# Expert blocks' rows by an indirect load from a scratch tensor instead of a one-hot product, and a signal of its own for the gate half

## The reference

```python
def clamped_swiglu(hgu):
    gate, up = jnp.split(hgu, 2, axis=-1)
    gate = jnp.minimum(gate, SWIGLU_LIMIT)
    up = jnp.clip(up, -SWIGLU_LIMIT, SWIGLU_LIMIT)
    return gate * jax.nn.sigmoid(SWIGLU_ALPHA * gate) * (up + 1)

xs = xt[row_tok].reshape(NB, MOE_BLOCK, D)      # the rows of each block's tokens
def expert_block(args):
    xb, e = args
    return clamped_swiglu(xb @ w1[e] + b1[e]) @ w2[e] + b2[e]
y = jnp.zeros((T, D)).at[row_tok].add(yb * row_gate[:, None])
```

## Time and profile before

| | |
|---|---|
| median of 3 runs | 2496.36 us (2496.22 to 2497.87) |
| the profiled execution | 2495.2 us |
| its span in the profile | 2493.4 us |
| PE, DVE, ACT, POOL busy | 94%, 42%, 25%, 2% |
| expert weights | 384 loads of 1 MB |

### The profile page before, as it was taken

The page is one execution under the profiler, slowest core; times in us unless marked ns, Lnnn a source line. Parts: engine busy times, 40 slices in busy tenths (PEclk is TensorE's granted clock), DMA queues, the critical chain, the costliest instruction groups (busy, mean ns, idle before and its releaser), DMA issues. The chain is left out here.

```text
span 2493.4 us, 30931 instructions
## 1 busy us (share of the span) xinstructions
PE 2344.1 (94%) x11448; PEld 1251.3 (50%) x11449; DVE 1040.7 (42%) x2256; ACT 633.7 (25%) x1451; POOL 46.0 (2%) x59
## 2 busy tenths in 40 slices
PE   7999899999999989899899789999999999999997
PEld 3545586468745558676786554333333333333332
DVE  3857542153600684766444433232233233223323
ACT  3006632343211353226331321111111111111111
POOL 0000010000000000000001000000000000000000
PEclk9999999999999999999999789999999999999999
DMA  9535611200112002763240149999998998998997
GB/s 374 201 135 203 233 68 43 91 11 35 70 67 80 22 1 101 255 217 136 68 169 34 63 163 405 417 381 377 417 417 350 417 417 348 417 417 346 418 418 307
DMA packets 154250, 567.96 MB, mean 228 GB/s; under 512 B 10832, under 2 KB 12368, under 8 KB 121136
## 3 DMA queue, kind: packets, MB, share of 16 engines
q1 hardware_dynamic: 154160, 566.75, 58.1%
HBM read 565.67 MB, written 1.05 MB: 227 GB/s over the span
## 5 line engine op out<-in xcount | busy, mean ns | idle before, releaser
L2596 PE MATMUL PS<-BIG,PW 128*64 128x512 f32 x2304 | 509.9, 597 | 10.6 <-DMA BIG<-in_w 10.6
L2596 PEld LDWEIGHTS PS<-BIG,PW 128*64 128x64 f32 x2304 | 160.6, 137 | 357.4 <-issue 323.6
L2622 PE MATMUL PS<-BIG,PW 128*64 128x512 f32 x1152 | 255.1, 595 | 8.6 <-ACT PW L2699 8.6
L2785 DVE TENSOR_SCALAR PW<-PS 128x512 f32<-128x512 f32 x36 | 24.9, 691 | 513.0 <-PE PS L2596 513.0
L2696 ACT ACTIVATE PW<-PW 128x512 f32<-128x512 f32 x36 | 22.7, 630 | 757.1 <-DVE PW L2785 757.1
L2622 PEld LDWEIGHTS PS<-BIG,PW 128*64 128x64 f32 x1152 | 79.3, 137 | 161.2 <-issue 144.1
L1062 PE MATMUL PS<-HT,BIG 128*128 128x512 f32 (+1 forms) x448 | 157.5, 507 | 0.0
L682 PE MATMUL PS<-HT,BIG 128*128 128x256 f32 x640 | 139.5, 379 | 2.1 <-PEq L794 2.1
L682 PEld LDWEIGHTS PS<-HT,BIG 128*128 128x128 f32 x640 | 121.4, 190 | 19.1 <-issue 2.7
L1062 PEld LDWEIGHTS PS<-HT,BIG 128*128 128x128 f32 x448 | 85.2, 192 | 65.5 <-issue 56.7
L1407 PE MATMUL PS<-BIG,HT 128*128 128x512 f32 x256 | 110.0, 592 | 0.0
(11 more groups left out here) (469 smaller groups left out, 3137.1 us busy)
## 6 DMA issues: line engine op xcount, KB each, us to landing
BIG<-in_w SPq DMA_DIRECT2D x384, 1024.0 KB, 15.7
BIG<-in_l_w_ada SPq DMA_DIRECT2D x24, 2048.0 KB, 8.3
BIG<-in_l_w_in SPq DMA_DIRECT2D x20, 2048.0 KB, 8.0
BIG<-in_w_ada SPq DMA_DIRECT2D x12, 2048.0 KB, 9.1
BIG<-in_l_w_out SPq DMA_DIRECT2D x8, 2048.0 KB, 8.2
BIG<-in_w_in SPq DMA_DIRECT2D x7, 2048.0 KB, 8.3
BIG<-in_w_out SPq DMA_DIRECT2D x2, 2048.0 KB, 8.1
BIG<-in_l_w_in SPq DMA_DIRECT2D x1, 1792.0 KB, 7.7
```

The source lines that it names most:

```text
L2596: ins = nc.tensor.matmul(PS[64 * g:64 * g + 64, 4 + half, :], xt[:, c % 4, c // 4, :], W[:, c, half * F + g * 512:half * F + g * 512 + 512 ...
L2622: ins = nc.tensor.matmul(PS[64 * g:64 * g + 64, 7, :], at_[:, k % 4, k // 4, :], W[:, 8 + k // 2, k % 2 * D + g * 512:k % 2 * D + g * 512 ...
```

## The change

The normed tokens are also stored to a scratch tensor `token_rows` in HBM, as 512 half rows of 2 KB. A table `row_of` of row numbers, 128 partitions x 49 block columns (MAX_BLOCKS + 1),, is made once: DVE splits each place into block and slot and writes `of_block` (some 18 small instructions, left out below), PE sums the table in 16 products and DVE adds the half-row offset. In the loop POOL copies the block's column of it and issues an indirect load of 128 half rows straight into `xg`, as soon as the rows before have been turned. From block 2 on this replaces the gather on PE, its copy on ACT and the tables on DVE. PE signals the end of the gate half of the first products before the up half of the last chunk, and DVE clamps the gate on that signal; the product with the sigmoid now comes first, and (up + 1) after it.

```diff
+            of_block = take(BIG, rest, 2, K, MAX_BLOCKS + 1)
+            row_of = take(BIG, rest, MAX_BLOCKS + 1).bitcast(U32)
+            row_now = take(BIG, rest, 1).bitcast(U32)
+            token_rows = nc.dram_tensor("token_rows", [2 * LAT, D // 2], F32)
...
+                    sp.wait_ge(*at("d_ready", 4))
+                    sp.dma_start(token_rows.rearrange("(n p g) d -> p n (g d)", n=2, p=P), htok).then_inc(loop["rows_stored"], 16)
...
+                @block.gpsimd
+                def _(pool):
+                    pool.wait_ge(loop["rows_stored"], 16)
+                    pool.wait_ge(loop["row_table_ready"], 1)
+                    n = trips(pool)
+                    with pool.Fori(2, n + 1) as i:
+                        pool.wait_ge(loop["gather_turned"], i)
+                        nc.gpsimd.tensor_tensor(turns[:, 0:1], ones[:, 0:1], ones[:, 0:1], ALU.add)
+                        nc.gpsimd.tensor_copy(row_now, row_of[:, bass.ds(i, 1)]).then_inc(loop["row_ready"], 1)
+                        pool.wait_ge(loop["row_ready"], i - 1)
+                        nc.gpsimd.tensor_tensor(turns[:, 1:2], ones[:, 0:1], ones[:, 0:1], ALU.add)
+                        nc.gpsimd.indirect_dma_start(out=xg, out_offset=None, in_=token_rows[:, :],
+                                                     in_offset=bass.IndirectOffsetOnAxis(ap=row_now, axis=0)).then_inc(loop["rows_landed"], 16)
...
-                    def turn_gathered(i):
+                    def turn_gathered(i, by_dma=True):
-                        pe.wait_ge(loop["gathered_copied"], i + 1)
+                        if by_dma:
+                            pe.wait_ge(loop["rows_landed"], i * 16 - 16)
+                        else:
+                            pe.wait_ge(loop["gathered_copied"], i + 1)
...
+                                if c == 7 and half == 0:
+                                    ins.then_inc(loop["gate_summed"], 1)
...
                     pe.wait_ge(loop["plan_copied"], 1)
+                    pe.wait_ge(loop["slots_split"], 1)
+                    for n in range(2):
+                        for k in range(K):
+                            for g in range(2):
+                                ins = nc.tensor.matmul(PS[64 * g:64 * g + 64, 7, 320:321 + MAX_BLOCKS], eq[:, n, k, :], of_block[:, n, k, :],
+                                                       start=(n + k == 0), stop=(n == 1 and k == K - 1))
+                    ins.then_inc(loop["rows_found"], 1)
...
                     pe.wait_ge(loop["gates_copied"], 1)
-                    second_products(0, 0)
+                    pe.wait_ge(loop["row_table_ready"], 1)
+                    second_products(0, 0, False)
...
-                    gather_next(1)
                     scatter_last(1)
...
                         first_products(i, load)
-                        gather_next(i)
                         scatter_last(i)
...
-                    with act.Fori(0, n) as i:
+                    one_block(0, False)
+                    with act.Fori(1, n) as i:
                         one_block(i)
...
                     tables(lambda x: x)
+                    dve.wait_ge(loop["pick_ready"], 3)
...
+                    ins.then_inc(loop["slots_split"], 1)
+                    link(ts(own[:, 2:3], const("partition"), float(SLOT), None, ALU.is_ge))
+                    dve.wait_ge(loop["rows_found"], 1)
+                    dve.wait_ge(loop["gates_copied"], 1)
+                    ts(row_of, PS[:, 7, 320:321 + MAX_BLOCKS], own[:, 2:3], None, ALU.add).then_inc(loop["row_table_ready"], 1)
...
                     def activation(i):
+                        dve.wait_ge(loop["gate_summed"], i + 1)
+                        nc.vector.tensor_scalar(gate_, PS[:, 4, :], 7.0, None, ALU.min).then_inc(loop["gate_clipped"], 1)
                         dve.wait_ge(used, i * 12 + 8)
-                        nc.vector.tensor_scalar(gate_, PS[:, 4, :], 7.0, None, ALU.min).then_inc(loop["gate_clipped"], 1)
                         nc.vector.tensor_scalar(up, PS[:, 5, :], 7.0, -7.0, ALU.min, ALU.max).then_inc(steps, 1)
-                        dve.wait_ge(steps, i * 8 + 5)
                         dve.wait_ge(loop["gate_clipped"], i + 1)
-                        nc.vector.scalar_tensor_tensor(up, up, 1.0, gate_, ALU.add, ALU.mult).then_inc(steps, 1)
-                        dve.wait_ge(steps, i * 8 + 6)
                         dve.wait_ge(loop["sigmoid_ready"], i + 1)
-                        nc.vector.tensor_tensor(act_, up, sig, ALU.mult).then_inc(loop["act_ready"], 1)
+                        nc.vector.tensor_tensor(gate_, gate_, sig, ALU.mult).then_inc(steps, 1)
+                        dve.wait_ge(steps, i * 4 + 6)
+                        nc.vector.scalar_tensor_tensor(act_, up, 1.0, gate_, ALU.add, ALU.mult).then_inc(loop["act_ready"], 1)
...
-                    dve.wait_ge(loop["gathered"], 2)
-                    tables(lambda x: 8 + x)
...
-                        dve.wait_ge(loop["gathered"], i + 2)
-                        tables(lambda x: i * 8 + (8 + x))
                         outputs(i)
```

More of the change, by code:

```diff
@@ L2402, in routed_experts @@
             norm_rows = take(BIG, rest, D)
+            of_block = take(BIG, rest, 2, K, MAX_BLOCKS + 1)
+            row_of = take(BIG, rest, MAX_BLOCKS + 1).bitcast(U32)
+            row_now = take(BIG, rest, 1).bitcast(U32)
+            turns = take(BIG, rest, 2)
+            token_rows = nc.dram_tensor("token_rows", [2 * LAT, D // 2], F32)
             pw = [0]
@@ L2436, in routed_experts @@
                 "act_copied y_copied scattered bias_used ranked order_ready plan_ready plan_turned plan_copied gate_exp_ready gates_ready gates_spread "
-                "places_ready places_copied gates_turned gates_copied bias2_scaled gather_turned xt_copied".split())}
+                "places_ready places_copied gates_turned gates_copied bias2_scaled gather_turned xt_copied gate_summed rows_stored "
+                "slots_split rows_found row_table_ready row_ready rows_landed".split())}
             with nc.Block() as block:
@@ L2600, in first_products @@
                                 beside()
-                    def gather_next(i):
-                        pe.wait_ge(loop["pick_ready"], i + 3)
-                        gather()
                     def scatter_last(i):
@@ L2609, in scatter_last, with second_products @@
                         scatter()
-                    def second_products(i, load):
+                    def second_products(i, load, by_dma=True):
                         pe.wait_ge(loop["act_ready"], i + 1)
@@ L2615, in second_products @@
                         ins.then_inc(loop["act_turned"], 1)
-                        turn_gathered(i + 1)
+                        turn_gathered(i + 1, by_dma)
                         pe.wait_ge(loop["act_copied"], i + 1)
@@ L2629, in _ @@
                     gather()
-                    turn_gathered(0)
+                    turn_gathered(0, False)
                     pe.wait_ge(loop["ranked"], 1)
@@ L2639, in _ @@
                     ins.then_inc(loop["gates_turned"], 1)
-                    gather_next(0)
+                    pe.wait_ge(loop["pick_ready"], 3)
+                    gather()
                     for n in range(4):
@@ L2692, in _, with one_block @@
                     copy_turned(0)
-                    def one_block(i):
+                    def one_block(i, by_dma=True):
                         act.wait_ge(loop["gate_clipped"], i + 1)
                         nc.scalar.activation(sig, gate_, ACT.Sigmoid, scale=1.702).then_inc(loop["sigmoid_ready"], 1)
-                        copy_gathered(i + 1)
+                        if not by_dma:
+                            copy_gathered(i + 1)
                         act.wait_ge(loop["act_turned"], i + 1)
@@ L2781, in _ @@
                     tables(lambda x: x)
+                    dve.wait_ge(loop["pick_ready"], 3)
+                    whole = own[:, 8:8 + 2 * K].bitcast(I32)
+                    link(nc.vector.tensor_copy(whole, flat(dest0)))
+                    link(ts(whole, whole, SLOT - 1, None, ALU.bitwise_and))
+                    link(nc.vector.tensor_copy(flat(dest), whole))
+                    for n in range(2):
+                        link(tt(eq[:, n, :, :], const("slot_row").unsqueeze(1).to_broadcast([P, K, SLOT]),
+                                dest[:, n, :].unsqueeze(2).to_broadcast([P, K, SLOT]), ALU.is_equal))
@@ new lines, in _ @@
+                    link(tt(dest, dest0, dest, ALU.subtract))
+                    link(ts(dest, dest, 1.0 / SLOT, None, ALU.mult))
+                    link(ts(own[:, 0:1], const("partition"), 2.0, None, ALU.mult))
+                    link(ts(own[:, 1:2], const("partition"), 2.0, float(2 * P), ALU.mult, ALU.add))
+                    for n in range(2):
+                        for k in range(K):
```

(12 more changed lines are left out.)

## The result

The changed kernel takes 2511.38 us (median of 4 runs, 2510.15 to 2513.31) against 2496.29 us for the kernel before beside it: 15.1 us slower, ratio 1.006 with a 95% interval of 1.0042 to 1.0077. The profiled execution has a span of 2508.9 us, 15.5 above the span of before. These are lines of the page of the changed kernel; they answer to the earlier trace rows; the fourth is new, and the last line is the kernel before's counterpart of the fifth.

The account below looks back on a forecast made before the run. The weight stream on the DMA engines (417 GB/s, 30.2 us an expert, plus stops) was taken as the bound; loads +20.4, start +2.3, stops -7.0, end -1.4 sum to +14.3 us, forecast 2510 us, range 2497 to 2530.

Parts of the forecast that it names:

- the terms 2.3 - 7.0 - 1.4: All but the loads: later start of the stream +2.3 us, shorter stops -7.0, shorter end behind the last chunk -1.4.
- the one distance that the forecast named: Time between two resumptions of SP's weight loading after stops, six experts apart: up from 192.0 to about 194.7 us.
- The price of a load: Each block's 262 KB indirect load takes 0.68 us of the 16 DMA engines; 30 count, +20.4 us.
- The free load: Rival: the loads ride beside the weight stream at no cost, so -6 us, 2490 us; chance 0.10.
- the dear one: Rival: POOL-written descriptors and an extra queue hold the engines up to 2.3 us a load, 2559 us; chance 0.07.
- The stops: At four halts of the weight stream PE comes 1.43 us earlier, -5.7 us; with another -1.3 at the first, -7.0.
- the catch-up at the first: At the stream's first stop PE will now have caught up after the start: another -1.3 us.
- The setup: Ahead of the loop, 16 products (3.5 us) and table work delay PE 3.7 us; the stream starts +2.3 us later.
- The end: Behind the last weight chunk, the rest of the kernel shortens by 1.4 us.
- The signal's failure: Rival: the gate half's early signal does not help and transposes start at the old time, 2517 us; chance 0.10.
- The fall of the clock: Rival: PE's waits in each chunk drop TensorE to half clock, 35 us at four stops and the end, 2545; chance 0.03.
- PE idle on DMA about 5 us per block: Sign expected in the profile: PE waits for weights before the first products, in place of 10.6 us in all.

Follow-up runs that it names:

- pair with half chunks: Only half of each weight chunk loaded from the second expert on: kernel before 2478.68 us (ratio 0.9933), changed kernel 2429.21 us (ratio 0.9731).
- none, one and two loads: Changed kernel with each indirect load of the loop removed, kept as it is, or issued twice: 2489.0, 2511.38 and 2530.05 us.
- plain loads by SP: Kernel before with one more SP load of 128 rows of 2 KB behind each expert's 12 chunks: 2513.32 us, ratio 1.0072.
- the kernel without loads: Changed kernel without the indirect load in the loop and the wait for it, xg keeping block 1's rows: 2489.0 us, ratio 0.9969.
- with the old activation: Kernel before with PE's gather moved behind chunk 3 of the first products, without the early gate signal: 2519.72 us, ratio 1.0094.
- the two profiles with the gather moved: Kernel before with PE's gather moved behind chunk 3 of the first products, plus the early gate signal: 2493.47 us, and 2494.18 us when repeated.

## Why the prediction was right

The forecast was 2510, measured 2511.4; its sum, +14.3 us, is what the loop stretch of the profiles shows. The mechanism held; that the number fits to 0.1 us is in part luck. By the loop stretches the loads cost 18.2 us where 20.4 were forecast, and everything else gave back 3.9 where the terms 2.3 - 7.0 - 1.4 make 6.1: two misses of 2.2 us that cancel. By the medians the two are 22.4 and 6.9.

- **What binds.** As predicted: the DMA at 417 GB/s between the stops, and distances between resumptions up by 3.1, 3.6 and 1.7 us, 8.4 in sum. The sum forecast for six, seven and six loads that count, less 1.43 at each stop, is 8.6; the one distance that the forecast named, at 2.7, is the one that fell shortest of it. The pair with half chunks shows it from the other side.
- **The price of a load.** Taken as 0.68 us from rows of the same width. The line through none, one and two loads gives 18 to 22 us for 30 that count, 0.6 to 0.75; the queue's 1.0% of the span gives 0.7 and the plain loads by SP 0.69. The free load (0.10) and the dear one (0.07) are both excluded. The Trainium skill ("DMA: Bandwidth & Descriptors", section "Anatomy of one DMA — SWDGE (gpsimd) path") gives a load about 2.0 us of fixed time and lays it to completion latency. The runs agree: held on the engines it would have made 78 us (the estimate of the forecast), and they show 18 to 22. The loads landed 7.0 us after issue, in a stretch with some 20 us to spare.
- **The stops.** They shrank by 42.4 - 33.3 = 9.1 us. Forecast were 7.0 by PE's gain and the catch-up at the first, and four loads hidden in them, 2.7 more: 9.7. Without the loads they shrank by 42.4 - 36.5 = 5.9, so the loads hid 3.2 us in them. PE's gain of 1.44 us a block was forecast as 1.43.
- **The setup, mis-sized.** Forecast +2.3 with 3.7 us of delay on PE. The changed kernel's start (PE):

```profile
1500.78 1.14 PE L2664 MATMUL PS<-BIG,PW 128*64 128x49 f32 x32
...
1507.72 0.60 PE L2637 MATMUL PS<-CONST,PW 128*128 128x128 f32 x4
...
1522.59 7.92 PE L2621 MATMUL PS<-BIG,PW 128*64 128x512 f32 x28
```

The 16 products took 1.14 us, not 3.5: I had halved the duration of one with its drain, but with 64 weight columns and 49 data columns their 32 records issue every 0.04 us. From expert 1's issue to the transposes it is 13.5 us, 1.0 more than before. Then a thing that I had not counted: some of the products after 1522.6 run at the 1.2 GHz level. This is the window, beside one of the loop (the kernel before has 1.00 in the first, as shown above):

```profile
1516.00:1528.00 12.00, 10.28 (x60) 5.61 (x60) 6.73 (x8) 0.00 (x0) 0.00 (x0) 0.86 0.98 377
```
```profile
2079.00:2096.00 17.00, 13.24 (x57) 3.39 (x56) 0.46 (x1) 0.00 (x0) 0.00 (x0) 1.00 1.01 417
```

Chunk 0 of block 1 is used 3.3 us after its first product where 2.1 were before, and SP issues expert 2 at 1525.86. The forecast was about 1526, 3.7 us of work later than before; it came so by 1.0 us of work, 1.1 of clock and 1.2 by which expert 1's issue itself was later in this profile (1494.2 against 1493.0). That time is right by luck. By the first resumption the whole start is +1.9, in which there are also the first stop, 2.9 us shorter, and the price of the first loads; without loads it is -0.6, as the forecast's 2.3 of setup less 2.7 at that stop makes -0.4.
- **The end.** Forecast -1.4 behind the last weights. These are the last expert's eighth chunk, before and after:

```profile
2466.01 1.94 PE L2596 MATMUL PS<-BIG,PW 128*64 128x512 f32 x8 [0.55 <-DMA BIG<-in_w]
```
```profile
2483.05 1.94 PE L2621 MATMUL PS<-BIG,PW 128*64 128x512 f32 x8 [0.55 <-DMA BIG<-in_w]
```

From there to the end of the span it is 27.4 us before and 25.9 after, 1.5 less; the kernel without loads also has 25.9. But from the last resumption to the end of the span it is 205.2 us against 201.3, and 201.1 with the loads taken away, only 0.2 less: between the resumption and the eighth chunk the kernel without loads took 1.3 us more than the kernel before (175.2 and 173.9), which the forecast did not have and whose cause is open.
- **The rivals.** The signal's failure (0.10) is excluded by the block's timeline, where the gate's clamp starts 0.85 us ahead of up's, which waits 0.17 us. The fall of the clock (0.03) did not come in the loop: 1.00, with DMA waits ahead of every chunk from 2079 to 2096. The example of the Trainium skill ("TensorE: Matmul & The Clock Gate", section "HAM oscillation — how this bites in real kernels") has waits of about 3 to 5 us between groups of products of about 2 us; here the groups take 1.77 us and the waits some 0.7, so the trace does not speak against it and shows only that waits this short kept the clock. It fell for a moment at the start. PE had just waited 1.7 us for DVE's copies there, but it waited 1.73 us at the same place in the kernel before, at 1.00, so that wait alone is not the cause. All six profiles of the changed kernel and its variants have 0.86 from 1516 to 1528. The cause is open.
- One reading was loose: "PE idle on DMA about 5 us per block". It fits a block in which PE has caught up with the stream, as the one from 2077 to 2096 (eight waits that read 4.1 us, 5.4 with the 0.17 of each). Over the 36 blocks it is 2.1 on average, the 74 us from above.

## What to carry to other kernels

Where two resources look full, find the one whose time adds up to the stretch: bytes divided by the rate between disturbances, plus the stops. Moving work from the other engine onto it lost here, though that engine saved some 50 us (the pair with half chunks). Putting the work inside the waits that the bound already causes adds no such price, but gained little here (1 to 4 us by the medians), as the other bound was near. And before taking away work that sits between a product and its activation, ask what it covers: with the old activation it covered 1 us a block.

## What the runs showed that was not expected

- A signal that was worth nothing (ratio 1.000) on one order of the same work was worth 26 us on another. A small edit's worth belongs to the schedule around it.
- The table load of the sigmoid disappears from ACT's loop. In the change the first block of that loop is written out ahead of it and the copy of the collected rows leaves it; which of the two does it was not tested. Before, from 1600 to 2400 us, it is

```profile
L2696 ACT ACT_TABLE_LOAD x29 | 37.2, 1283 | 0.5
```

and in the changed kernel none. It had stood beside PE's work; no run tells what it was worth.
- TensorE's clock at the start differs by kernel, and between two executions of one: 1.00 from 1520 to 1544 before, 0.91 and 0.86 in the two profiles with the gather moved, which there went with 4.6 and 4.1 us lost up to the first resumption. Its cause was not settled.
